# A kernel of two transformer blocks: TensorE repeats no constant product ahead of a wait

## The reference

```python
def rmsnorm(x, g):
    xf = x.astype(jnp.float32)
    y = xf * lax.rsqrt(jnp.mean(xf * xf, axis=-1, keepdims=True) + EPS)
    return (y * g.astype(jnp.float32)).astype(x.dtype)
...
def first_block(...):
    for i in range(DEPTH):
        ...
        hx = rmsnorm(x, norm_g[i, 0]) * (1.0 + sc_x) + sh_x
        hc = rmsnorm(ctx, norm_g[i, 0]) * (1.0 + sc_c) + sh_c
        ...                                  # i == 0: conv_module, i == 1: attention_module
        x = x + g_x * rmsnorm(yx, norm_g[i, 1])
        fx = rmsnorm(x, norm_g[i, 2]) * (1.0 + scf_x) + shf_x
        x = x + gf_x * rmsnorm(swiglu(fx, ffn_w1[i], ffn_w3[i], ffn_w2[i]), norm_g[i, 3])
        ...
def second_block(...):
    for l in range(DEPTH):
        mix = token_mixing(x, w_in[l], ...)
        x = layer_norm(ALPHA * x + mix, ln1_g[l], ln1_b[l])
        ffn = conv_ffn(x, ffn_w_up[l], ffn_conv_w[l], ffn_conv_b[l], ffn_w_down[l])
        x = layer_norm(ALPHA * x + ffn, ln2_g[l], ln2_b[l])
```

## Time and profile before

| | |
|---|---|
| runs of the kernel before | 1945.77, 1947.14, 1947.43 us; median 1947.14 |
| the profiled execution's own time | 1945.2 us |
| its span | 1943.4 us |
| mean granted clock of TensorE | 0.985 of full speed |
| TensorE busy | 1870.2 us |
| VectorE, ScalarE, GpSimd busy | 1303.3, 955.2, 519.5 us |

### The profile page before, as it was taken

The page is one execution under the profiler, slowest core; times in us unless marked ns, Lnnn a source line. Parts: engine busy times, 40 slices in busy tenths (PEclk is TensorE's granted clock), DMA queues, the critical chain, the costliest instruction groups (busy, mean ns, idle before and its releaser), DMA issues.

```text
span 1943.4 us, 35606 instructions
## 1 busy us (share of the span) xinstructions
PE 1870.2 (96%) x14432; PEld 1664.9 (86%) x14432; DVE 1303.3 (67%) x2518; ACT 955.2 (49%) x1711; POOL 519.5 (27%) x663
## 2 busy tenths in 40 slices
PE   6999999999999979999998999999999999999998
PEld 3865787887877947999988999899999899989997
DVE  4998898553747865645578655684748775567473
ACT  4414632232224576544456564564655566456464
POOL 0200100000001443100012223737372322364745
PEclk9999999999999989999999999999999999999999
DMA  9345267642631302455545445455554543545551
GB/s 352 132 142 185 88 209 250 210 167 96 226 111 54 112 19 87 152 185 184 184 153 176 141 138 167 163 174 184 185 165 161 176 142 129 174 142 185 190 179 55
DMA packets 84546, 307.28 MB, mean 158 GB/s; under 512 B 9376, under 2 KB 10656, under 8 KB 84128
## 3 DMA queue, kind: packets, MB, share of 16 engines
q1 hardware_dynamic: 84384, 305.01, 46.5%
HBM read 303.92 MB, written 1.05 MB: 157 GB/s over the span
## 4 chain that ended last, share of the span: by engine, by line
PE 85%; DVE 8%; ACT 3%; issue 1%; DMA 1%; POOL 1%; SPq 0%; DVEq 0%; ACTq 0%; POOLq 0%
PE pb L599 18%; PE pb L601 18%; PE pb L600 18%; PE pb L572 6%; PE pb L578 6%; PE pb L573 6%; PE pb L840 2%; DVE wlo L2030 2%; ACT whi L1337 1%; DMA raw<-wstream 1%; PE pb L1003 1%; POOL wlo L3007 1%; PE pb L651 1%; PE pb L1208 1%; PE pb L625 1%
## 5 line engine op out<-in xcount | busy, mean ns | idle before, releaser
L599 PE MATMUL pb<-Hh,whi 128*128 128x256 f32 (+1 forms) x2288 | 696.4, 304 | 1.6 <-DVE SM L2634 1.4
L601 PE MATMUL pb<-Hh,wlo 128*128 128x256 f32 (+1 forms) x2288 | 689.2, 301 | 0.0
L600 PE MATMUL pb<-Hl,whi 128*128 128x256 f32 (+1 forms) x2288 | 689.2, 301 | 0.0
L1337 ACT ACTIVATE whi<-raw 128x1024 fp32r<-128x1024 f32 x468 | 489.3, 1053 | 329.2 <-PE pb L601 161.7
L2030 DVE TENSOR_TENSOR wlo<-raw,whi 128x1024 fp32r<-128x1024 f32 x330 | 430.0, 1310 | 253.7 <-ACT whi L1337 253.1
L3007 POOL TENSOR_TENSOR wlo<-raw,whi 128x256 fp32r<-128x256 f32 x552 | 413.7, 785 | 690.0 <-ACT whi L1337 689.3
L599 PEld LDWEIGHTS pb<-Hh,whi 128*128 128x128 f32 x2288 | 436.6, 191 | 25.2 <-issue 3.5
L601 PEld LDWEIGHTS pb<-Hh,wlo 128*128 128x128 f32 x2288 | 436.7, 191 | 15.1
L600 PEld LDWEIGHTS pb<-Hl,whi 128*128 128x128 f32 x2288 | 436.8, 191 | 14.8
L3031 POOL TENSOR_TENSOR X<-X,tmpb 128x512 f32<-128x512 f32 (+1 forms) x21 | 23.9, 1138 | 581.0 <-DVE tmpb L2196 580.9
L572 PE MATMUL pb<-Hh,whi 128*128 128x256 f32 (+1 forms) x544 | 164.4, 323 | 4.0 <-ACT Hh L1410 2.1
(11 more groups left out here) (349 smaller groups left out, 2962.9 us busy)
## 6 DMA issues: line engine op xcount, KB each, us to landing
raw<-wstream SPq DMA_DIRECT2D x572, 512.0 KB, 3.5
X<-xin SPq DMA_DIRECT2D x2, 1024.0 KB, 8.6
out<-X SPq DMA_DIRECT2D x8, 128.0 KB, 1.8
CON<-consts SPq DMA_DIRECT2D x1, 957.5 KB, 8.1
VEC<-vecs SPq DMA_DIRECT2D x1, 694.0 KB, 8.5
CON<-consts SPq DMA_DIRECT2D x1, 147.0 KB, 4.0
VEC<-vecs SPq DMA_DIRECT2D x1, 88.0 KB, 1.9
```

What stands on the lines that cost most here:

```text
L599: e.matmul(dst, hi, xh, start=k == 0, stop=False)
L600: e.matmul(dst, hi, xl, start=False, stop=False)
L601: i = e.matmul(dst, lo, xh, start=False, stop=k == kt - 1)
L1337: e.activation(whi[:, s % NPIECE, :], raw[:, p % NRAW, :], ACT.Copy).then_inc(sig("act_hi", ("hi", p)), 1)
```

## The change

All calls of `warm` go, and with them the function and the argument `idle`. Nothing is put in their place. In `singles` and `zlin`, whose lines are left out below, only the argument goes. The diff, with lines of context left out:

```diff
-            def warm(dst, n):
-                w.wait_ge(*con_in)
-                for _ in range(n):
-                    e.matmul(dst[:, 0:256], con("ident"), CON[:, coff["ident"]:coff["ident"] + 256], start=True, stop=True)
-
-            def lin_first(keys, kt, src, n, high, low, until=None, between=lambda k: None, idle=0, short=()):
+            def lin_first(keys, kt, src, n, high, low, until=None, between=lambda k: None, short=()):
                 got = [bank("pm", ("lin",) + key, *(until(key) if until else [("ev",) + key])) for key in keys]
-                warm(got[0], idle)
...
-            def lin(keys, kt, src, n, xon, until=None, between=lambda k: None, idle=0):
+            def lin(keys, kt, src, n, xon, until=None, between=lambda k: None):
...
-                warm(got[0], idle)
...
-            def widen(S, n, *until, ring="pt", r=None, idle=0):
+            def widen(S, n, *until, ring="pt", r=None):
                 b = bank(ring, ("spread", S), *until)
-                warm(b, idle)
...
-                if root is None:
-                    warm(b, 1)
...
-                widen(S, n, ("rdone", R, 7), idle=1)
+                widen(S, n, ("rdone", R, 7))
...
-            singles([("pw1", 2 * j + s) for j in range(8) for s in range(2)], FIRST, 8, H2, 512, hh("n0"), hx("n0"), between=second, idle=3)
+            singles([("pw1", 2 * j + s) for j in range(8) for s in range(2)], FIRST, 8, H2, 512, hh("n0"), hx("n0"), between=second)
...
-            widen("y0", 512, ("rdone", "r0", 7), idle=2)
+            widen("y0", 512, ("rdone", "r0", 7))
...
-                    lin_first(ups[:FIRST], 8, src, n, hh(S), hx(S), idle=5 if l == pi == 0 else 0)
+                    lin_first(ups[:FIRST], 8, src, n, hh(S), hx(S))
...
-            lin_first([("k", 0), ("k", 1)] + early, 8, H2, 512, hh("n2"), hx("n2"), idle=4, short=early)
+            lin_first([("k", 0), ("k", 1)] + early, 8, H2, 512, hh("n2"), hx("n2"), short=early)
...
-            widen_halves("y2", ("rdone", "r2", 7), 1)
-            widen_halves("r2", ("mt", "n3", 7), 1)
+            widen_halves("y2", ("rdone", "r2", 7))
+            widen_halves("r2", ("mt", "n3", 7))
...
-                lin_first([("z", l, key) for key in dd[:4]], 8, XS, T, xhi, xon, lambda key: [("ev",) + key], idle=2 if l else 3)
+                lin_first([("z", l, key) for key in dd[:4]], 8, XS, T, xhi, xon, lambda key: [("ev",) + key])
...
-                    singles(ups, FIRST, 8, XS, T, lambda k: [("lnh", l, 1, k)], lambda k: [("lnl", l, 1, k)], idle=0 if pi else 2)
+                    singles(ups, FIRST, 8, XS, T, lambda k: [("lnh", l, 1, k)], lambda k: [("lnl", l, 1, k)])
```

More of the change, by code:

```diff
@@ L605, in lin, with singles @@
                     between(k)
-            def singles(keys, first, kt, src, n, high, low, between=lambda k: None, idle=0):
-                lin_first(keys[:first], kt, src, n, high, low, between=between, idle=idle)
+            def singles(keys, first, kt, src, n, high, low, between=lambda k: None):
+                lin_first(keys[:first], kt, src, n, high, low, between=between)
                 for key in keys[first:]:
@@ L1042, in tensor, with widen_halves @@
                 token_halves(slots.at(("sq", "y2b", k)), 128, False, k == 7, ("sums", "y2c") if k == 7 else ("xsum", "y2b", k))
-            def widen_halves(S, until, idle):
+            def widen_halves(S, until):
                 b = bank("pt", ("spread", S), until)
-                warm(b, idle)
                 w.wait_ge(*on("rec", S))
@@ L1062, in tensor, with zlin @@
                 xhi = (lambda k: [("xph", k)]) if l == 0 else (lambda k: [("lnh", 0, 2, k)])
-                def zlin(*keys, idle=0):
-                    lin([(key[0], l) + key[1:] for key in keys], 8, XS, T, xon, lambda key: [("ev",) + key], idle=idle)
+                def zlin(*keys):
+                    lin([(key[0], l) + key[1:] for key in keys], 8, XS, T, xon, lambda key: [("ev",) + key])
                 dd = [("dk", m) if s == 0 else ("dq", m) for m in range(4) for s in range(2)]
-                lin_first([("z", l, key) for key in dd[:4]], 8, XS, T, xhi, xon, lambda key: [("ev",) + key], idle=2 if l else 3)
+                lin_first([("z", l, key) for key in dd[:4]], 8, XS, T, xhi, xon, lambda key: [("ev",) + key])
                 for key in dd[4:]:
```

## The result

The changed kernel took 1950.24 us, the median of 11 runs (1946.03 to 1952.36), the kernel before 1945.37 us beside it (11 runs, 1944.26 to 1947.43). The ratio is 1.0020 with a 95% interval of 1.0011 to 1.0030, that is +3.9 us (+2.1 to +5.8), just about the bound of 0.2%. The forecast was +5.4, or 1952.5 us in a range of 1948.5 to 1957.0. That time stood on a median of 1947.14 from three runs; eleven runs of the kernel before give 1945.37, so 1.8 of the 2.3 us by which 1952.5 is too high belong to the base and not to the change.

What follows compares the result with a forecast made beforehand. TensorE was taken to pace nearly all the time. Losses of 6.9 us at sites 2 to 8, less 1.5 at site 1, gave +5.4 on 1947.1: 1952.5 us, range 1948.5 to 1957.0.

Steps and rivals of the forecast that it cites:

- Site 1: At pw1, 3 calls: real work can start at 28.08 in place of 30.58 us; a gain of 1.5 us.
- Sites 2, 3 and 4: y0 and first feed-forward; keys; y2 and r2: more half clock costs 0.7 and 0.8, little changes at the last, 0.2 us.
- site 3: Keys, 4 calls: half clock lasts to 627 or 631 us, VectorE hides part; cost 0.8 us.
- Sites 5 and 6: r3 with first projection, and first up-projection: without the calls the clock falls; costs 1.8 and 1.1 us.
- Site 7: Second projection, 2 calls: 0.3 us comes back, half clock lasts longer for 1.4; net cost 1.1 us.
- One stretch more: At the second projection, the half clock from 1453.4 us lasts another stretch without the calls, losing 1.4 us.
- Site 8: Second up-projection, 2 calls: clock falls for about 3.4 us of dense work, 1.4 us, part hidden; cost 1.2.
- The half clock costs less: Rival, 23%: half clock ends sooner or costs less at the sites; +1.5 us in all, 1948.6 us.
- Removed work was on the path and the clock holds: Rival, 5%: pw1's 2.50 us and the second projection's up to 2.02 us return whole; 1942.6 us.
- Every site pays the longest stretch: Rival, 7%: 2.9 us each at sites 5 to 8, 1.5 each at 2 to 4; +14.6, up to 1961.7 us.

Runs made afterwards that it cites:

- e2: Kernel before with all 26 repeated products kept but 16 columns wide in place of 256; 1953.31 us against 1943.89, ratio 1.0037.
- e7: Changed kernel with only the calls of r3 and the second block's first projection put back; 1949.87 us against 1945.48 for the kernel before, ratio 1.0023.
- e1: Kernel before without only the 3 calls ahead of pw1; 1943.42 us against 1943.89, ratio 0.9995.
- e4: Kernel before without only the 13 calls at y0, first feed-forward, keys, y2 and r2; 1946.77 us, ratio 1.0006, +1.2 us.
- e9: The kernel before, unchanged, timed and profiled a second time; 1943.27 us against 1945.05, ratio 0.9996.
- e8: The changed kernel, unchanged, timed and profiled once more; 1951.76 us, ratio 1.0033 against the kernel before.
- e5: Kernel before without pw1's calls, with two calls added ahead of three layer norms' broadcasts; 1941.98 us against 1945.48, ratio 0.9985.
- e10: The same program as e5, timed and profiled again; 1940.61 us against 1945.05 for the kernel before, ratio 0.9977.
- e6: e5 with calls also added in the first block's norms; 1942.21 us against 1945.48 for the kernel before, ratio 0.9984.

## Why the prediction was right

**The mechanism** is shown three times over: the half-clock stretches stand where it put them (974.8, 1258.1, 1742.8 us for 975.6, 1259 and 1740); e2 keeps the instructions and loses the clock, and the time goes with the clock; e7 returns one site's calls, and that site's loss is gone while those of sites 6, 7 and 8 stay. The mean clock was foreseen at about 0.975 and is 0.978, or 0.9786 over 16 runs of the changed kernel, against 0.9858 over 77 runs of before.

**Site 1**, -1.5: the means say -1.4; by the times alone it isn't told from nothing (e1).

**Sites 2, 3 and 4**, 0.7, 0.8 and 0.2: 0.8, 1.1 and 0.2. At site 3 the half clock lasts to 630.08, the later of the two ends that the prediction named, and TensorE idles 3.56 us ahead of the first slice. By the times, e4's +1.2 us and its interval hold the forecast's 1.7.

**Sites 5 and 6**, 1.8 and 1.1: 2.1 and 1.2. At site 5 the stretch is the long one in all three profiles without calls. At site 6 I took 3.4 us of half clock and it was 6.8; but before isn't always at full clock there, as e9 shows, and the two errors nearly cancel. That this term fits is luck: against the first profile of before, which the prediction read, e8 loses 2.0 us there.

**Site 7**, 1.1: 0.8. Three of four profiles without calls have the half clock for 3.4 us, as long as before, and lose 0.5; the one read here first has it for 6.8 us, and lost 1.4. "One stretch more" holds in one execution in four. In the other three the stretch is no longer than before but lies later: in e8 from 1463.21, with real work from 1463.17, so that all of it falls on the first slices and 3.4 x 0.43 = 1.5 us are lost, where before only the work from 1456.17 to 1456.85 was at half (0.3 us). Against that the first slice starts 0.59 us earlier in them, as the broadcast ahead of it now runs at full clock (1.07 us in place of 1.66). The 0.3 us credited for the calls themselves was too much: before, the first product started at 1456.17, 0.14 us behind its slice of Hh.

**Site 8**, 1.2, is the term that was mis-sized. The half clock behind the norm lasted 6.83 us, not "about 3.4 us", with 5.46 us of TensorE's work in it, and cost 2.3 us against the first profile of before. The step that failed is "the clock falls, for about 3.4 us of dense work: 1.4 us each". What was missing in it is the broadcast. The fall came at 1742.82, just ahead of it, and it takes 1.94 us (L762) in place of 1.07: 0.9 us that the step did not count. The dense work is as the step has it: real work runs from 1746.12 on, 3.5 us of it at the half clock, and 3.5 x 0.43 = 1.5 us; the 6.8 us make 2.4. In e7, where the stretch was 3.41 us, the site cost 1.0 (its shift of -0.34 holds -1.34 from ahead of the norm), close to what was forecast. The rest of the 3.0 in the table isn't the change: two of the four profiles with the calls lack 1.4 us of a wait ahead of the site and the half-clock stretch that follows it, of which the last section tells. Among the profiles that have both that wait and that stretch, those without the calls lose 2.2 us against those with them.

**The sum.** The eight differences add up to 7.8 us, more than the +3.9 and +6.4 of the times. Of that, 0.8 us is site 8's wait, just told, and a part is chance in so few profiles. A further part may be real: a half-clock stretch near 1051 us (1.4 us) is in 6 of the 8 profiles with site 5's calls and in none of the 4 in which they were out or short. That would take 1.0 us from the loss; whether the one fall prevents the other was not tried.

**The rivals.** "The half clock costs less" (+1.5) is below the interval of both measurements of the whole. "Removed work was on the path and the clock holds" is out: sites 5 to 8 fell in every profile without calls. "Every site pays the longest stretch" came true in stretches at sites 2, 3, 5, 6 and 8 of the first profile, and at 7, but 2.9 us for one was too dear: it cost 2.3 us at site 5 and at site 8. At site 5 the fall is at 974.82 and real work starts at 976.46; the 1.6 us between cost little, and the 5.2 us behind it 5.2 x 0.43 = 2.2.

## What to carry to other kernels

Products without use that TensorE does while it waits can be worth their place: look at what the granted clock does just behind them, and whether real work was ready when they ran; where the clock was low anyway (site 1) they cost time, where it was held (site 5) four calls of them were worth some 2 us. The same calls with 16 columns in place of 256 were worth nothing. And before a difference of 0.2% is explained from two traces, profile each kernel twice: one site of the same program moved by 2.7 us.

## What the runs showed of the hardware that was not expected

**A VectorE instruction with two durations sets a wait of TensorE.** At 1721 us VectorE computes one `wlo` (L2030, 128x1024) while GpSimd computes others (L3007) over the whole of that time. In the timeline of VectorE, and then of TensorE, of the first profile of before:

```profile
1720.81 3.23 DVE L2030 TENSOR_TENSOR wlo<-raw,whi 128x1024 fp32r<-128x1024 f32 x1
...
1729.51 1.10 PE L1285 MATMUL pb<-tmpb,CON 128*32 128x64 f32 x24 [1.69 <-ACT tmpb L1910]
```

and of e9, the same program:

```profile
1720.99 1.84 DVE L2030 TENSOR_TENSOR wlo<-raw,whi 128x1024 fp32r<-128x1024 f32 x1
...
1728.31 0.92 PE L1285 MATMUL pb<-tmpb,CON 128*32 128x64 f32 x20 [0.32 <-ACT tmpb L1910]
```

The timeline of GpSimd over the same time, in the first profile of before and in e9:

```profile
1711.77 11.19 POOL L3007 TENSOR_TENSOR wlo<-raw,whi 128x256 fp32r<-128x256 f32 x16 [2.21 <-ACT whi L1337]
...
1711.94 12.19 POOL L3007 TENSOR_TENSOR wlo<-raw,whi 128x256 fp32r<-128x256 f32 x16 [2.21 <-ACT whi L1337]
```

In all 12 profiles 3.2 us goes with a wait of 1.7 us (nine) and 1.8 us with one of 0.3 us (e4, e5, e9); the change doesn't decide which. In two of the nine (e7, e10) the wait was not followed by a half-clock stretch, in seven it was, and in none of the three: so one instruction's duration brings 1.4 us, and with the fall 2.7. The three with 1.8 us are also those in which one of GpSimd's pieces takes 1.7 us in place of 0.7, so that its 16 pieces take 12.2 us in place of 11.2. So in each profile one of the two engines takes longer while both work, VectorE in nine and GpSimd in three. What decides which was not tried.

**Half clock is not time lost.** The clock of all timed runs (0.9858 and 0.9786 of full speed, which is a share of 2.8% and 4.3% at the half clock) makes 55 and 83 us of it in an execution, 28 us more. The time is 4 to 6 us longer, and 5 to 8 us if the 1.4 us that site 1 gives back are added: 0.19 to 0.28 us for each microsecond at half. Much of the added half clock lies in waits. In the first profile after, sites 2 and 3 have 6.83 us more of it each, in stretches of 10.24 and 13.66 us of which TensorE is busy 6.46 and 8.96, and lose 0.9 and 1.1 us; site 5 has the same 6.83 us more, three quarters of them with work ready, and loses 2.3. At site 2 the first profile of before has a stretch of 3.41 us that e9, e5 and e6 do not have, and they are only 0.1 us earlier for it. And e6 has a mean clock of 0.9905 to e5's 0.9875, some 12 us less at half, and the same time. The Trainium skill (TensorE: Matmul & The Clock Gate, "Terms") puts the penalty at the throttled time times (1 - K/N), where K/N is the granted share of the clock, one half here. By it 28 us would cost 14 us (an estimate). The trace does not agree, since TensorE has idle time in them.

**Where the clock falls differs between executions of one program**, by the stretches near 1051 and 1256 us. The same page of the Trainium skill ("What's actually happening") has the chip's reckoning run free of the kernel's start. The three pairs of profiles of one program (before and e9, after and e8, e5 and e10) agree with that: each pair differs in the place or the length of its falls.
